# Score matmuls of the window attention: two banks in turn, or one bank after the other

## What is computed

```
n_chunks = seq // CHUNK                       # 256 // 64 = 4 chunks
kb = _band(k, n_chunks)                       # each chunk sees its own 64 keys and the 64 before
s = einsum('bcqhgd,bckhd->bhgcqk', qc, kb) * (64 ** -0.5)
s = where(valid, s, -inf)                     # chunk 0 has no chunk before it
m = maximum(max(s, axis=-1), sink)
p = exp(s - m);  p = p / (sum(p) + exp(sink - m))
o = einsum('bhgcqk,bckhd->bcqhgd', p, vb)
```

## Time and profile before

| | |
|---|---|
| median of three runs | 2292.81 us |
| profiled execution | 2292.81 us |
| span of its profile | 2291.1 us |
| PE busy | 2272.7 us, 99% |
| PE weight loads busy | 1880.4 us, 82% |
| DVE busy | 1271.0 us, 55% |
| ACT busy | 1007.5 us, 44% |
| the mixer's layer-0 window attention | about 199 to 296 us of the span |

### The profile page before, as it was taken

One profiled execution on the slowest core, in us unless ns is written; L12 is line 12 of the kernel. 1 busy time (PEld: TensorE's weight loads), 2 busy tenths in 40 slices (PEclk: granted clock), 3 DMA queues, 4 the chain that ended last, 5 costly groups with the idle time before them and its releaser, 6 DMA issues.

```text
span 2291.1 us, 29587 instructions
## 1 busy us (share of the span) xinstructions
PE 2272.7 (99%) x10710; PEld 1880.4 (82%) x10710; DVE 1271.0 (55%) x1498; ACT 1007.5 (44%) x1242; POOL 55.9 (2%) x85
## 2 busy tenths in 40 slices
PE   8999999999999999999999999999999999999999
PEld 6888888888888888888888888888888888888887
DVE  6756665555555554444556666665555555554443
ACT  5656544444444443344443434344444444443332
POOL 2101000000000000000000000000000000000000
PEclk9999999999999999999999999999999999999999
DMA  7564446666666665655554545456666666666664
GB/s 247 171 201 128 131 156 195 189 189 189 190 186 190 192 184 178 193 185 185 175 145 144 164 147 165 147 184 184 192 187 189 189 187 192 185 191 195 199 193 130
DMA packets 213277, 410.29 MB, mean 179 GB/s; under 512 B 13264, under 2 KB 13516, under 8 KB 213196
## 3 DMA queue, kind: packets, MB, share of 16 engines
q1 hardware_dynamic: 212108, 407.11, 58.8%
q10 hardware_dynamic: 1088, 2.10, 0.2%
HBM read 407.06 MB, written 2.10 MB: 179 GB/s over the span
## 4 chain that ended last, share of the span: by engine, by line
PE 92%; DVE 1%; issue 0%; ACT 0%; POOL 0%; DVEq 0%; ACTq 0%
PE unit_bank L1364 86%; PE mix_bank L1385 2%; PE mix_bank L1520 2%; PE mix_bank L1451 0%; PE mix_bank L1414 0%; DVE w_lo L833 0%; PE mix_bank L1423 0%; PE mix_bank L1505 0%; DVE tanh_q L1065 0%; PE mix_bank L1460 0%; PE mix_bank L1435 0%; PE mix_bank L1549 0%; PE mix_bank L1547 0%; PE mix_bank L1540 0%; PE mix_bank L1530 0%
## 5 line engine op out<-in xcount | busy, mean ns | idle before, releaser
L833 DVE TENSOR_TENSOR w_lo<-raw,w_hi 128x1024 fp32r<-128x1024 f32 x768 | 936.9, 1225 | 826.9 <-ACT w_hi L488 817.2
L488 ACT ACTIVATE w_hi<-raw 128x1024 fp32r<-128x1024 f32 x768 | 810.5, 1060 | 973.0 <-PE unit_bank L1364 947.7
L1364 PE MATMUL unit_bank<-w_hi,hT_hi 128*128 128x512 f32 (+1 forms) x1984 | 778.0, 392 | 0.0
L1364 PE MATMUL unit_bank<-w_hi,hT_lo 128*128 128x512 f32 (+1 forms) x1984 | 771.2, 389 | 0.0
L1364 PE MATMUL unit_bank<-w_lo,hT_hi 128*128 128x512 f32 (+1 forms) x1984 | 770.2, 388 | 0.0
L1364 PEld LDWEIGHTS unit_bank<-w_hi,hT_lo 128*128 128x128 f32 x1984 | 372.4, 188 | 77.1
L1364 PEld LDWEIGHTS unit_bank<-w_lo,hT_hi 128*128 128x128 f32 x1984 | 372.7, 188 | 74.0
L1364 PEld LDWEIGHTS unit_bank<-w_hi,hT_hi 128*128 128x128 f32 x1984 | 372.6, 188 | 74.1 <-issue 0.3
L1364 PE MATMUL unit_bank<-w_hi,gT_hi 128*128 128x512 f32 x704 | 279.5, 397 | 0.0
L1364 PE MATMUL unit_bank<-w_hi,gT_lo 128*128 128x512 f32 x704 | 279.1, 396 | 0.0
L1364 PE MATMUL unit_bank<-w_lo,gT_hi 128*128 128x512 f32 x704 | 279.0, 396 | 0.0
(11 more groups left out here) (227 smaller groups left out, 1114.7 us busy)
## 6 DMA issues: line engine op xcount, KB each, us to landing
raw<-in_w_gate_up SPq DMA_DIRECT2D x352, 512.0 KB, 4.2
raw<-in_w_down SPq DMA_DIRECT2D x176, 512.0 KB, 4.5
raw<-in_w_in_b SPq DMA_DIRECT2D x104, 512.0 KB, 4.3
raw<-in_w_o SPq DMA_DIRECT2D x64, 512.0 KB, 4.0
raw<-in_w_in_a SPq DMA_DIRECT2D x40, 512.0 KB, 3.9
raw<-in_w_mem_kv SPq DMA_DIRECT2D x32, 512.0 KB, 4.5
mem_tok<-in_mem SPq DMA_DIRECT2D x4, 512.0 KB, 8.8
x_tok<-in_x SPq DMA_DIRECT2D x4, 512.0 KB, 8.5
```

The costliest lines, as they stand in the source:

```text
L488: act.activation(w_hi[:, s, :, :], raw[:, s, :, :], ACT.Copy).then_inc(sems["hi_ready"], 1)
L833: dve.tensor_tensor(w_lo[:, s, :, :], raw[:, s, :, :], w_hi[:, s, :, :].bitcast(F32), ALU.subtract).then_inc(sems["lo_ready"], 1)
L1364: ins = pe.matmul(unit_bank[2 * pair + tile][:, 0:cols], a, b[:, s, j, 0:cols], start=opens and n == 0 and j == 0 and m == 0, stop=closes ...
```

## The change

Only `scores` on PE changes; the same matmuls with the same operands are issued, in another order. Before, the loops went over the heads outside and over the two banks inside, with all matmuls of shape A first and B or M behind them, and both semaphores rose at the end. Now the loop over banks is outside: the wait for the bank's `free` semaphore, all of the bank's matmuls, and its `full` semaphore, then the other bank. In `scores(1)`, A and B of a head stand directly behind each other.

```diff
-                    rows = {2: slice(0, HD_A), 3: slice(HD_A, 2 * HD_A)}
-                    for n in range(4):
-                        for b in (2, 3):
-                            r = rows[b]
-                            pe.matmul(mix_bank[b][:, n * P:(n + 1) * P], qT[r, n, s * P:(s + 1) * P],
-                                      kT[r, g, s * P:(s + 1) * P], start=True, stop=True)
-                    early = {}
-                    if s == 0:
-                        for b in (2, 3):
+                        for n in range(4):
+                            h = 2 * n + b - 2
+                            r = slice((b - 2) * HD_A, (b - 1) * HD_A)
+                            if s == 0:
+                                ins = pe.matmul(mix_bank[b][:, n * P:(n + 1) * P], qT[r, h // 2, 0:P], kT[r, g, 0:P],
+                                                start=True, stop=True)
+                                continue
+
+
+                            pe.matmul(mix_bank[b][:, n * P:(n + 1) * P], qT[r, h // 2, P:2 * P], kT[r, g, P:2 * P],
+                                      start=True, stop=True)
+                            ins = pe.matmul(mix_bank[b][0:64, n * P:(n + 1) * P], qT[r, h // 2, P:P + 64],
+                                            kT[r, g, 64:64 + P], start=True, stop=True)
+                        if s == 0:
                             r = slice((b - 2) * HD_A, (b - 2) * HD_A + 1)
-                            early[b] = pe.matmul(mix_bank[b][0:P // 2, :].rearrange("p (h k) -> p h k", h=4)[:, :, P // 2:P],
-                                                 ones_row[r, :], masked_row[r, :, :], start=True, stop=True)
-                    else:
-                        for n in range(4):
-                            for b in (2, 3):
-                                r = rows[b]
-                                early[b] = pe.matmul(mix_bank[b][0:64, n * P:(n + 1) * P], qT[r, n, P:P + 64],
-                                                     kT[r, g, 64:64 + P], start=True, stop=True)
-                    for b in (2, 3):
-                        early[b].then_inc(sems[f"full{b}"], 1)
+                            ins = pe.matmul(mix_bank[b][0:P // 2, :].rearrange("p (h k) -> p h k", h=4)[:, :, P // 2:P],
+                                            ones_row[r, :], masked_row[r, :, :], start=True, stop=True)
+                        ins.then_inc(sems[f"full{b}"], 1)
```

More of the change, by code:

```diff
@@ L1409, in scores @@
                         t.move(f"free{b}")
-                    if not window:
-                        for b in (2, 3):
+                        if not window:
                             for n in range(2):
@@ L1416, in scores @@
                             ins.then_inc(sems[f"full{b}"], 1)
-                        return
-                    rows = {2: slice(0, HD_A), 3: slice(HD_A, 2 * HD_A)}
-                    for n in range(4):
-                        for b in (2, 3):
-                            r = rows[b]
-                            pe.matmul(mix_bank[b][:, n * P:(n + 1) * P], qT[r, n, s * P:(s + 1) * P],
-                                      kT[r, g, s * P:(s + 1) * P], start=True, stop=True)
-                    early = {}
```

## The result

The changed kernel takes 2318.49 us, median of four runs (2318.24 to 2320.54), against 2292.87 for the kernel before: the ratio is 1.0113 with a 95% interval of 1.0101 to 1.0125. The direction was as forecast, but 2318.5 lies above the range: 25.6 us were added where 16.4 were predicted. The profiled execution has a span of 2317.7 us, 26.6 more than before.

The account below looks back on a forecast made before the run. PE was taken to bound the kernel, with nothing hidden: scores(1) adds 4.12 us a call and scores(0) 1.35, three calls each, 16.4 us onto 2292.81, giving 2309.2 us; range 2303 to 2313.

Parts of the forecast that it names:

- PE bounds the kernel and nothing hides its added work: Whole kernel: PE busy 2272.7 of 2291.1 us; no PE wait absorbs the added time, gain at most 0.7 us.
- DVE does start earlier on bank 2: DVE's L930: reduces bank 2 while PE fills bank 3, `minus_max` up to 0.7 us sooner, gain put at nothing.
- The three figures: PE's `scores`: 0.11 us a step of one tile, first record 0.21 (A) or 0.16 (B), 0.20 leaving a shape.
- Rivals 1, 2 and 3: `scores`: cheap shape changes, 2300.6, 0.09 with its half form; tiles overlap anyway, 2292.8, 0.05; own loads exposed, 2312.8, 0.03.
- One reading behind them: L1463: `v_mid` at 227.32 and `kv_a` at 227.33 taken to show that paired records come one from each tile.
- PE's clock 1.00: Sign expected in the timeline after: PE's granted clock stays at 1.00.
- busy PE up by some 16 us: Sign expected in the profile after: PE's busy time grows by some 16 us.
- The sum: `scores` on PE, three calls of each half: 3 x (4.12 + 1.35) = 16.4 us added.
- rival 4: Added stretches of `scores`: PE slows where work is sparser, some 14 us more, 2323; chance 0.03.

Follow-up runs that it names:

- the kernel with both tiles: Against the kernel before, scores(1) alternates A and B after every head with both tiles side by side, scores(0) as before: 2296.36 us, ratio 1.0013.
- the experiment with twice the work: Against the kernel before, scores(1) alternates A and B per head, both tiles side by side, the whole set done twice: 2305.81 us, ratio 1.0056.

## Why the prediction missed

- *PE bounds the kernel and nothing hides its added work.* Right. PE's wait for L914 is still there, as in the earlier trace rows: `PE mix_bank L1385 <- DVE q_a L914: 0.7, 2, 0.5` (us in total, times, longest). DVE does start earlier on bank 2, as foreseen, and gains nothing. Its timeline after, beside the earlier trace rows:

```profile
203.76 0.69 DVE L930 TENSOR_REDUCE top<-mix_bank 128x4 f32<-128x512 f32 x1 [1.24 <-PE mix_bank L1432]
205.17 0.69 DVE L930 TENSOR_REDUCE top<-mix_bank 128x4 f32<-128x512 f32 x1 [0.72 <-PE mix_bank L1432]
```

- *The three figures, step 0.11, entry 0.21 and 0.16, exit 0.20.* Right to 0.01 us with one tile active, so `scores(0)` at 2.68 and `scores(1)` at 6.2 came out as worked, and so did their sum: 4.0 measured alone, 12.7 in the kernel that has the longer `scores(1)` at full clock. Rivals 1, 2 and 3 are out by the same rows: no change of shape was cheaper, no records of two tiles started together, and blocks ran at 0.11. One reading behind them was of another case than `scores`: the two tiles of the earlier trace rows are halves of the array's columns (`128*64`), not of its rows. That the row halves run side by side is shown by the kernel with both tiles, whose four records take the same 0.42 us as two of one tile.
- *The clock.* This is the step that failed, and of the signs that I gave "PE's clock 1.00" and "busy PE up by some 16 us" (it was 26.2) went with it. The sum priced every added step at the full clock and left the fall to rival 4 with a chance of 0.03. What I set against it was the earlier trace rows: half of 1.5 us idle, clock at 1.00. That is one short stretch between dense ones; it doesn't speak for 6.2 us in which the array works little all along, and none of the earlier trace rows shows such a stretch. The right reading would have been that the trace can't bound this, and a chance and a range to match. I also took "PE busy" for work: the busy share was 100% in the earlier trace rows, and stayed at 100% here, while the records stood 0.16 to 0.21 us apart where those of one shape are 0.11 apart.
- *Rival 4's size.* Its pace was right, its place wrong. A unit of A and B at the lower clock takes 1.34 us, 0.56 more, where it had 0.6. But it had the added stretches at that pace from start to end, +14 us. The falls came late in each call and lasted into the full-array matmuls behind, so 9.2 us were added over the forecast (10.4 in the profiled execution), most of them not in the lines that changed.

The Trainium skill, "TensorE: Matmul & The Clock Gate", section "Why this matters for your kernels", advises against idle gaps of PE between bursts of matmuls if throughput is not to drop mid-kernel. Here it dropped without one: the rows show PE busy for 6.00 of 6.00 us ahead of the first fall. The Trainium skill, "Trainium Kernel Development and Optimization", section "Performance Expectations", calls matmul busy time a bad measure of how near a kernel is to its roofline, because matmuls are pipelined. The trace agrees, and the two windows in the experiment with twice the work show it: 7.16 of 7.16 with 34 records at a clock of 0.84, 6.30 of 6.30 with 65 at 1.00.

What stays open: why the third fall of the changed kernel lasted some 10 us, its others 7 and some of other kernels 3.3, and which of several equal stretches brings a fall. The traces show when the clock fell, not what the chip counted.

## What to carry to other kernels

When a change thins out TensorE's work, compare how many records of the same size run in a microsecond before and after, not busy shares (the 512-column records of L1364 stand 0.23 us apart at full clock, so numbers of unlike records don't compare). Look up the granted clock in windows around the place, and in more than one run; if no stretch of the old trace is as thin for as long, its clock can't be taken from it. Matmuls on half of the array belong side by side with those on the other half, and matmuls of one shape belong together: each pair of records that no longer runs side by side costs 0.11 us here, and a change of shape 0.16. A result that is overwritten later may also cost a shape: here dropping it gave 3.7 us, and each other order that was tried made the kernel slower.

## What the runs showed of the hardware that was not expected

- The clock fell to its lower level three times while PE counted as busy throughout, each time behind A and B of one tile in turn; a fall of some 7 us cost 2.9 to 3.2 us, of which 2.1 of the 3.1 read in one trace were paid by the full-array matmuls behind it, and one of 3.3 us cost 1.7.
- It didn't fall behind 4.2 us of one tile in blocks, nor behind 6.3 us of both tiles in turn.
- Four quarter tiles, of which two each have the same rows and the same bank, ran side by side: 32 records in 1.04 us.
- What the clock costs varies from run to run of one kernel: with one group changed, six runs took 2300.4 to 2300.7 us at a mean clock of 0.998 and two 2298.5 or 2298.6 at 0.999.
